# Gate and up of a routed expert layer with the weights as stationary operand

## What is computed

```python
def expert_choice_ffn(h, w_router, w_gate, w_up, w_down):
    ...
    aff = jax.nn.softmax(jnp.dot(xs, w_router).astype(jnp.float32), axis=-1)
    cap = EC_FACTOR * n // N_EXPERTS
    gates, idx = lax.top_k(aff.T, cap)
    xe = xs[idx]
    hid = jax.nn.silu(jnp.einsum('ecd,edf->ecf', xe, w_gate)) * jnp.einsum('ecd,edf->ecf', xe, w_up)
    ye = jnp.einsum('ecf,efd->ecd', hid, w_down) * gates[..., None].astype(h.dtype)
    out = jnp.zeros_like(xs).at[idx.reshape(-1)].add(ye.reshape(-1, D))
```

## Time and profile before

| | us |
|---|---|
| median of three runs | 1894.52 (1892.17 to 1896.1) |
| the profiled execution | 1889.44, span 1887.7 |
| PE busy / weight loads busy | 1794.9 (95%) / 973.2 (52%) |
| DVE / ACT / POOL busy | 815.6 / 316.3 / 200.5 |
| expert stage, layer 0 / layer 1 | about 433 to 955 / 1365 to 1888 |

### The profile page before, as it was taken

One profiled execution on the slowest core, in us unless ns is written; L12 is line 12 of the kernel. 1 busy time (PEld: TensorE's weight loads), 2 busy tenths in 40 slices (PEclk: granted clock), 3 DMA queues, 4 the chain that ended last, 5 costly groups with the idle time before them and its releaser, 6 DMA issues. The chain is left out here.

```text
span 1887.7 us, 33944 instructions
## 1 busy us (share of the span) xinstructions
PE 1794.9 (95%) x14602; PEld 973.2 (52%) x14602; DVE 815.6 (43%) x1746; ACT 316.3 (17%) x680; POOL 200.5 (11%) x275
## 2 busy tenths in 40 slices
PE   5999989988999999999889999899799999999996
PEld 2455655443466565445345666554435655653553
DVE  2335876254242424343343458843534342424241
ACT  2223643120000000000032245521200000000000
POOL 1004200000000000000010142000000000000000
PEclk9999999999999999999999999999999999999998
DMA  9860020358999999999985300331699999999993
GB/s 385 311 234 1 1 109 32 163 208 346 395 410 398 408 401 409 404 405 401 392 316 218 134 0 1 109 133 69 250 390 408 401 398 398 401 396 406 399 404 116
DMA packets 56213, 526.70 MB, mean 279 GB/s; under 512 B 12046, under 2 KB 13694, under 8 KB 26142
## 3 DMA queue, kind: packets, MB, share of 16 engines
q1 hardware_dynamic: 40494, 375.60, 49.8%
q10 hardware_dynamic: 9312, 128.45, 16.1%
q0 software_dynamic: 6336, 21.63, 4.6%
HBM read 503.91 MB, written 24.38 MB: 280 GB/s over the span
## 5 line engine op out<-in xcount | busy, mean ns | idle before, releaser
L643 PE MATMUL PS<-arena,xe 128*32 128x512 f32 x3456 | 384.9, 600 | 11.4 <-DMA arena<-w_exp 7.6
L643 PE MATMUL PS<-ada,xe 128*32 128x512 f32 x2688 | 294.4, 592 | 4.2 <-DVE RA L1491 4.2
L643 PEld LDWEIGHTS PS<-arena,xe 128*32 128x32 f32 x3456 | 168.0, 111 | 214.2 <-issue 175.2
L659 PE MATMUL PS<-arena,hdT 128*32 128x512 f32 x1536 | 268.0, 596 | 5.6 <-DVE RA L1511 3.9
L661 PE MATMUL PS<-arena,hdT 128*32 128x256 f32 x1024 | 264.7, 381 | 0.0
L643 PEld LDWEIGHTS PS<-ada,xe 128*32 128x32 f32 x2688 | 130.5, 110 | 158.7 <-issue 121.9
L1168 ACT ACTIVATE RA<-PS 128x768 f32<-128x768 f32 x32 | 25.9, 810 | 975.5 <-PE PS L643 975.5
L1478 DVE STREAM_TRANSPOSE RA<-RA 32x256 f32<-32x256 f32 x384 | 167.1, 435 | 40.5 <-DMA RA<-normed_rows,idx_g 34.8
L703 PE MATMUL PS<-arena,RB 128*128 128x512 f32 (+1 forms) x480 | 183.4, 530 | 0.0
L1491 DVE TENSOR_TENSOR RA<-RA,PS 128x768 f32<-128x768 f32 x32 | 30.5, 954 | 339.4 <-ACT RA L1168 339.4
L664 PE MATMUL PS<-arena,hdT 128*32 128x256 f32 x1536 | 157.8, 381 | 0.0
(11 more groups left out here) (293 smaller groups left out, 1846.1 us busy)
## 6 DMA issues: line engine op xcount, KB each, us to landing
arena<-w_exp SPq DMA_DIRECT2D x76, 2048.0 KB, 20.9
arena<-w_exp ACTq DMA_DIRECT2D x60, 2048.0 KB, 14.2
ada<-w_exp SPq DMA_DIRECT2D x56, 2048.0 KB, 21.4
arena<-ada_rest SPq DMA_DIRECT2D x16, 2048.0 KB, 9.2
ada<-ada_first SPq DMA_DIRECT2D x8, 2048.0 KB, 33.8
arena<-w_in SPq DMA_DIRECT2D x4, 2048.0 KB, 10.1
arena<-w_out SPq DMA_DIRECT2D x2, 4096.0 KB, 12.7
arena<-w_in SPq DMA_DIRECT2D x4, 1536.0 KB, 18.8
```

The costliest lines, as they stand in the source:

```text
L643: last = mm(PS[GRP * q:GRP * (q + 1), g * 512:(g + 1) * 512], xe[:, k, GRP * g:GRP * (g + 1)], w[:, q, :], start=(k == 0), stop=(k == KD - ...
L659: mm(PS[GRP * q:GRP * (q + 1), 1536:2048], tok(q), w[:, 0:512], start=first, **flags)
```

## The change

Gate and up take the weights as stationary operand, 128x128 at a time, sixteen blocks `f` (eight of gate, eight of up), and move the 80 tokens. Gate lands in PSUM banks 0 and 1, up in banks 2 and 3, features on the partitions, so SiLU and product write the hidden vectors in the form that down needs: `hidden_turned` and its semaphore go. Two buffers take turns (`hdT` and a part of RA), down reads the one of its expert and moves to banks 4 and 5. VectorE clears the 16 spare columns of both buffers, ahead of the first gather. The loops of ACT and VectorE run over pairs of experts. In the last layer the gate and up weights of expert 15 go to `ada1` as expert 13 frees it, and its down weights go by SP to `arena[:, 0:8192]` as expert 14's gate and up free it. The host lays the weights out to match.

```diff
@@ where weights go, SP @@
-                gate_up_parts(first + 15, False, first + 14)
                 if l + 1 < LAYERS:
+                    gate_up_parts(first + 15, False, first + 14)
                     first_modulation(l + 1, (2, 3))
+                else:
+                    gate_up_parts(first + 15, True, first + 13)
+                    for j in range(2):
+                        sp.wait_ge(gu_used.sem, 4 * (first + 14) + (j + 1))
+                        sp.dma_start(arena[:, j * 4096:(j + 1) * 4096],
+                                     w_exp[bass.ds(first + 15, 1), (4 + j) * P:(5 + j) * P, :].rearrange("a p n -> (a p) n")
+                                     ).then_inc(ewa_in[j].sem, 16)
@@ gate_up, PE @@
-                    for g in range(3):
-                        for q in range(4):
-                            last = mm(PS[GRP * q:GRP * (q + 1), g * 512:(g + 1) * 512], xe[:, k, GRP * g:GRP * (g + 1)],
-                                      w[:, q, :], start=(k == 0), stop=(k == KD - 1), skip_group_check=True)
+                    for f in range(16):
+                        o = (f // 4) * 512 + (f % 4) * SLOT
+                        last = mm(PS[:, o:o + SLOT], w[:, f, :], xe[:, k, 0:SLOT],
+                                  start=(k == 0 and f % 4 == 0), stop=(k == KD - 1), skip_group_check=True)
@@ down, PE @@
-                pe.wait_ge(hd_rdy.sem, E + 1)
+                pe.wait_ge(hm_rdy.sem, E + 1)
...
-                    tok = lambda grp: hdT[:, k, GRP * grp:GRP * (grp + 1)]
+                    tok = lambda grp: hidden[odd][:, k, GRP * grp:GRP * (grp + 1)]
@@ SiLU, ACT @@
-                if not isinstance(E, int) or E:
-                    act.wait_ge(hd_rdy.sem, E)
-                A(hid, PS[:, 0:1536].rearrange("p (g c) -> p g c", g=3)[:, :, 0:REST], ACT.Silu).then_inc(sg_rdy.sem, 1)
+                A(hid[odd], gu_view(0), ACT.Silu).then_inc(sg_rdy.sem, 1)
@@ product, DVE @@
-                V.tensor_tensor(hid, hid, PS[:, 0:1536].rearrange("p (g c) -> p g c", g=3)[:, :, REST:512], ALU.mult).then_inc(hm_rdy.sem, 1)
+                V.tensor_tensor(hid[odd], hid[odd], gu_view(1), ALU.mult).then_inc(hm_rdy.sem, 1)
-            def hidden_turned(E):
-
-                dve.wait_ge(hm_rdy.sem, E + 1)
-                dve.wait_ge(dn_used.sem, 2 * E + 1)
-                V.transpose(hdT[:, :, :].rearrange("p b (g s) -> p g b s", g=3),
-                            hid.rearrange("p g (b r) -> p g b r", r=GRP)).then_inc(hd_rdy.sem, 1)
@@ ahead of the first gather, DVE @@
-                V.memset(xe[:, :, SLOT:PAD], 0.0)
+                dve.wait_ge(stored.sem, stored.at(l, 2 * NT))
+                for h in hidden:
+                    V.memset(h[:, :, SLOT:PAD], 0.0)
```

More of the change, by code:

```diff
@@ L645, in gate_up, with down @@
                     if k % 2:
                         last.then_inc(gu_used.sem, 1)
-            def down(E):
+            def down(E, odd, spare=None):
                 pe.wait_ge(ys_rdy.sem, E + 1)
-                pe.wait_ge(hd_rdy.sem, E + 1)
+                pe.wait_ge(hm_rdy.sem, E + 1)
                 for k in range(KD):
-                    if k % 4 == 0:
+                    if k % 4 == 0 and spare is None:
                         pe.wait_ge(ewd_in[k // 4].sem, E * 16 + 16)
-                    w = down_weights(k)
+                    elif k % 4 == 0:
+                        pe.wait_ge(ewa_in[k // 4].sem, spare)
+                    w = down_weights(k, spare is not None)
@@ L660, in down @@
                     for grp in range(2):
[L661 removed]
+                        mm(PS[96:P, 2048 + grp * REST:2048 + (grp + 1) * REST], tok(grp), w[:, MAIN:D],
                            start=first and grp == 0, **flags)
                     for q in range(3):
[L664 to L665 removed]
+                        mm(PS[GRP * q:GRP * (q + 1), 2560:2816], tok(q), w[:, 512:MAIN], start=first, **flags)
@@ L666, in down @@
+                    last = mm(PS[96:P, 2560:2816], tok(2), w[:, MAIN:D], start=first, **flags)
                     if k % 4 == 3:
@@ L1119, in _ @@
                     first_modulation(l + 1, range(4))
-                down(l * EXP + EXP - 1)
                 if l + 1 < LAYERS:
+                    down(l * EXP + EXP - 1, 1)
                     first_modulation(l + 1, range(4, KD))
+                else:
+                    down(l * EXP + EXP - 1, 1, (l * N_A + N_A) * 16)
                 pe.wait_ge(ys_rdy.sem, ys_rdy.at(l, EXP))
@@ L1390, in down_parts @@
                                       ).then_inc(ewd_in[j].sem, 16)
[L1392 to L1396, removed]
+                silu_gate(l * EXP, 0)
+                with act.Fori(0, N_B) as i:
+                    E = l * EXP + 2 * i
+                    silu_gate(E + 1, 1)
+                    down_parts(E + 1)
+                    silu_gate(E + 2, 0)
+                    down_parts(E + 2)
+                silu_gate(l * EXP + EXP - 1, 1)
+                if l + 1 < LAYERS:
+                    down_parts(l * EXP + EXP - 1)
         @block.vector
@@ L1937, in _, with one_expert @@
                 tokens_in(l * EXP)
-                times_up(l * EXP)
-                hidden_turned(l * EXP)
+                times_up(l * EXP, 0)
                 first.end()
-                with dve.Fori(1, EXP) as e:
+                def one_expert(e, odd):
                     E = l * EXP + e
@@ L1945, in _ @@
                     column(loop, l, e + 2, 1, idx_g[:, :], idx_rdy)
-                    times_up(E)
+                    times_up(E, odd)
                     tokens_in(E)
-                    hidden_turned(E)
                     rows_out(l, e - 1, E - 1)
                     loop.end()
+                with dve.Fori(0, N_B) as i:
+                    one_expert(2 * i + 1, 1)
+                    one_expert(2 * i + 2, 0)
+                one_expert(EXP - 1, 1)
                 if l + 1 < LAYERS:
@@ L2134, in expert_slabs @@
     u = w_up.reshape(n, 4, 2, P, FF).transpose(0, 1, 3, 2, 4)
-    d = w_down.reshape(n, 4, KD, GRP, D).transpose(0, 2, 1, 3, 4).reshape(n, 2, 4, P, D).transpose(0, 1, 3, 2, 4).reshape(n, 2, P, 4096)
-    gu = np.concatenate([w[..., q * REST:(q + 1) * REST] for q in range(4) for w in (g, u)], axis=-1)
+    d = w_down.reshape(n, 2, 4, P, D).transpose(0, 1, 3, 2, 4).reshape(n, 2, P, 4096)
+    gu = np.concatenate([g, u], axis=-1)
     return np.concatenate([gu.reshape(n, 4, P, 4096), d], axis=1).reshape(n, 6 * P, 4096)
```

34 lines of the change are left out of this document (20 added, 14 removed).

## The result

The changed kernel takes **2220.1 us** (2194.96 to 2222.54), the kernel before beside it on the same chip 1895.31: a ratio of 1.1687 [1.1648, 1.1726]; both times are medians of four executions. The direction was as forecast, 2135 (2108 to 2165) was too low by 85 us. The profiled execution took 2222.54, 333.1 over that of before. One of the four took 2194.96, 24 to 28 us less than the others, at a mean granted clock of 0.962 where they have 0.950 to 0.951.

What follows compares the result with a forecast made beforehand. PE (TensorE) sets the loop's pace, with DMA close behind. Terms 253.8 - 10.8 - 1.7 - 0.5 + 0.3 give +241 us, on the median of 1894.5 us 2135.5 us; range 2108 to 2165.

Steps and rivals of the forecast that it cites:

- Gate and up, +253.8: Gate and up on PE: 256 records at 0.1116 us, 28.57 us instead of 20.64 per expert, +253.8 us over 32.
- the L703 and L825 rows over the transpose: Price of a gate and up record: 0.1112 and 0.1118 us from full-load matmuls, not 0.074 from the gather's transpose.
- Joints: Range allowance where a full load meets a step of four: 7 us either way, 0.2 us an expert.
- Clock, "I take no change": PE's clock in gate and up: stays at 1.00, as in the stretch with L825's bursts; no time added.
- sum of 2130.5: Forecast counted from the profiled execution of the kernel before, 1889.44 us, instead of from the median.
- rival B: Clock falls in gate and up because the array streams little: 57.2 us each, 3050 us in all; chance 0.03.
- Weights on time, -10.8 and -1.7: First layer's sixteenth expert: its weights no longer late, normal period, -10.8 us; down's w_exp wait gone, -1.7 us.
- some 0.85: Sign to look for: DMA's share falls to some 0.85.
- Small terms: SiLU and product shrink to about 0.68 and 0.80 us, exposed after expert 0: -0.5 us; an added memset: +0.3 us.
- as before: Sign at the kernel's end: the last 27 us (down, VectorE's rows, the scatter) look unchanged.
- C: Gate and up's loads and matmuls don't overlap: 0.179 us a record, 45.7 us an expert, 2684 us; chance 0.02.
- A: Moving side sets gate and up's price: 0.074 us a record, DMA the bound, 1885 us in all; chance 0.05.

Runs made afterwards that it cites:

- move128: Changed kernel with 128 moving columns instead of 80 in gate and up (96 for the last k), the extra results unread; 2145.07 us, ratio 1.1315.
- move32: Changed kernel with only 32 moving columns in gate and up, 48 of the 80 tokens left out; 2897.68 us, one execution.
- load64: Changed kernel with 64 of each block's 128 weight columns loaded in gate and up, 80 still moving; 1890.59 us, one execution.

## Why the prediction was right or wrong

**Gate and up, +253.8: right.** The changed kernel's records at full clock start 0.112 us apart, and move128 shows that the moving side has no part in it. The choice of the L703 and L825 rows over the transpose was the right one. What is over the forecast comes under Joints.

**Clock, "I take no change": this is the step that failed**, for 81 of the 92 us by which the profiled execution lies above its sum of 2130.5. L825's bursts at clock 1.00 were taken as evidence for gate and up, and they last 3.8 us at most, with other matmuls between them, where this stream runs for 28 us on its own. The prediction put this down against itself in rival B, but had only two answers there, no gate and up slow or all 32. There is a third, and the trace of before had its beginning: pauses ahead of gate and up, and at the first of them a clock of 0.51 for 3 us. The missing question was who lifts it again. Behind that pause of the kernel before it was gate and up themselves, with 512 moving columns, within 3.4 us; with the change they don't, and 3 of 32 stay at half clock whole: 3 x 26 us, and some 3 us in the downs that lift the clock. That is B's price in a tenth of its places, but not B's mechanism. B had the stream itself bring the clock down; in the changed kernel it never did (every gate and up that was running at full clock stayed there to its end), it only failed to bring it back. That B's mechanism exists is shown by move32. How many gate and ups would be slow could not be read from the trace of before: in it the clock fell at the first pause of each layer and not at the second, in the changed kernel at the first of layer 0 and the second of layer 1.

**Joints, inside the range but one-sided.** Down's first start to the next gate and up's first start, in layer 1 of the changed kernel, against the earlier trace rows:

```profile
1711.65 0.63 PE L674 MATMUL PS<-arena,hdT 128*32 128x512 f32 x3
...
1722.15 1.01 PE L655 MATMUL PS<-xe,arena 128*128 128x80 f32 x7
```

10.50 us instead of 10.32. Of the 0.35 us a period this joint gives 0.18, 6 us in all, where 7 either way had been allowed; the way into down and the load interval (0.112 for 0.1116) give the rest, 5 us, where 15 had been allowed for the interval. What in the hand-over costs this was not tried.

**Weights on time, -10.8 and -1.7: right.** SyncE's transfers land 7.9 us (500:620, early in layer 0) and 10.1 us (1720:1780, the same stretch as in the earlier trace rows) after their issue:

```profile
DMA to landing us min/median/max: 7.5/7.9/10.2
...
DMA to landing us min/median/max: 7.7/10.1/12.0
```

DMA's share in the loops is 0.91 to 0.93, forecast "some 0.85" (higher, with the same bytes, but no longer behind), PE waits 0.2 us for w_exp in all, and expert 15 of layer 0 costs a normal period. **Small terms:** SiLU is 0.70 us (0.68 forecast), the product 0.82 (0.80); the pauses shrank from 2.12 to 1.91 us as put down, and the end behind the last SiLU is 3.5 us shorter, at clock 0.85 in the last 31 us where the earlier trace rows has 0.68; "as before" was wrong by that.

**Rivals.** C is excluded by 0.112 us with 128 moving columns. The sentence on row groups (the Trainium skill, TensorE: Matmul & The Clock Gate, section The mechanism), by which C would hold, is contradicted by move128 as by the earlier trace rows. The prediction passed over that the same section also lets a load go ahead when it targets the background weight buffer; with that these runs would agree, but which of the two happens no run here shows. A is excluded at full load width, and load64 shows that its 1885 was about the right size for the case.

**Without the pauses** the forecast of 2135.5 stands beside 2139.69. By the profiled executions it is 2130.5 beside 2139.31, 9 us, mostly the 11 of joints and loads less what the end gave back; that the medians lie only 4 apart is in part the 5 us by which before's profiled execution was under its median.

## What to carry to other kernels

In this kernel a matmul of 128 loaded columns costs its load, 0.112 us a record, with 80 and with 128 moving columns alike; so count the loaded columns before the moving ones. And then ask of such a stream not only whether it holds the clock, but whether it could lift it: search ahead of each long stretch for a pause in which the clock falls, and price the whole stretch at half speed if nothing dense stands between. Filling such a pause pays where the stream behind it can't lift the clock (80 us here) and not where it can (nothing in the kernel before), and instructions added ahead of a long loop can bring pauses of their own, so keep the count, or read the waits of issue afterwards.

## What the hardware showed beyond that

- One and the same stream of loads with 80 moving columns runs for 54.5 us at clock 0.50 and for 28.5 us at 1.00, busy for 100% of both: the level depends on what stood before it. With 32 moving columns it falls without a pause; with 128 it stays at 1.00 behind the same pause of 1.91 us, or falls and is back within 4.5 us; with 80 and half of the columns loaded it is back within 3 us.
- A pause of 1.91 us was enough to bring the clock down at two of four places. At a third the clock was low already and the pause changed nothing; at the fourth, ahead of gate and up 0 of layer 1, it stayed up. What sets the places apart is open.
- 20 instructions more ahead of each loop, 40 in all ahead of the second, with no other change, cost 172 us between the medians (2220.1 to 2392.6) and 150 by the two ratios: five pauses at heads of passes of the second loop, 27 us, each brought a gate and up at half clock, and layer 1's gate and up 0 was slow too. Single executions lie 61 us apart (2349.61 to 2410.43).
- Fillers in the same two pauses made the changed kernel 80 us faster (the loops left in their place) or 148 us slower (moved by 20 instructions for each filler ahead of them). At 2139.69 us the best form of the change remains 13% behind the kernel before.
